# A two-layer transformer block on one core: out's products and the latent attention's projections laid between attention units

## The chip, the cores and the metric

The kernel runs on one core of a Trainium2 chip. The metric is the device time of one execution in microseconds (us); the time of a kernel is the median of its runs.

## The reference

One sequence of 256 tokens, width 1024, goes through two layers, all in fp32. Each layer is a mixer and a mixture of experts, with `x = layer_norm(ALPHA * x + h)` behind either.

- **Mixer of layer 0**: 16 heads of 64. Eight are *sliding* heads (window 128, with sinks). Eight are *NSA* heads, a gated sum of three branches: compressed keys, selected blocks (with 256 tokens all blocks are selected, so a causal attention), and a window of 512 (again causal). The 16 heads' outputs, 1024 columns, are multiplied by `w_out` (1024 x 1024).
- **Mixer of layer 1** (multi-head latent attention): x is projected to 384 + 256 + 32 columns; the first two are RMS-normed latents, from which `w_uq` gives q (16 heads of 64 + 32) and `w_ukv` gives keys without position (64 each) and values (64 each). The last 32 of q and of k are rotated by position; the 32 of k are shared by all heads. Causal attention, then `w_out`.
- **Experts**: 64 experts of inner width 256, six picked per token through groups, and one shared expert. All 64 experts' weights, three times 1024 KB each, are read in each layer, 2 x 201 MB of the 444 MB that the kernel moves.

## The kernel before

Tokens are worked in two blocks of 128 (`TC` = 2), the width in eight chunks of 128 (`KC`). `xrow` holds x by rows, `xcol` its transpose. Each engine has its instruction list in the order of the source and waits by semaphores; nothing is reordered by a planner, so the lists written out in `@block.tensor` (L887), `@block.scalar`, `@block.vector` (L1353) and `@block.sync` (L428) are the schedule. SyncE (SP) issues all DMAs, each behind the waits that stand before it.

**Memory.** `ring` has four slots of 3 MB, one expert each; in the mixers they hold weights and data of the mixer (slot 0 `win1`, then q by rows, `qn1`; slot 1 `w_ukv`; slot 2 `w_uq`; slot 3 latents and turned queries). `wbig` holds `w_out` (`wout`) in a mixer, 4 MB, and in `wbig`'s first half stand the first four units' probabilities of layer 0. PSUM has eight banks, `BANK[0..7]`, in pairs `PS[0..3]`. The expert weights are refilled by `refills` (L347, L350): gate and up of a slot once TensorE has used it (`gu_pe`), down likewise. Before the expert stage slots 0 to 3 and one kept expert are loaded: in layer 0 behind the projections, in layer 1 slot 2 after the q products, slot 1 after the kv products, slot 0 after the turned queries and keys; slot 3, the shared expert and the kept one in `mixture_loads` (L406), behind the last values.

**Attention units.** A unit is four heads by 128 queries. For unit u TensorE makes the scores (`pe_scores`, L572), VectorE masks them and takes the maximum (`soften`, L1465, L1468), ScalarE takes exponentials with sums (`act_exp`, L1134), VectorE normalises (`normalise`, L1545, L1551), TensorE turns the probabilities (`pe_turn_probs`, L613), ScalarE copies them out of PS[2] (`act_turned`, L1148), and TensorE multiplies by the values (`pe_values`, L598 and L586). Units of the first query block see 128 keys, those of the second 256. VectorE copies the heads' outputs to `attot`, and `pe_out_part` (L637) multiplies by `wout` into `OUT` = (PS[0], PS[3]), one for each token block, in two halves of 512 columns, each the sum of eight products over 128 rows.

**Layer 0** has 12 units: 0 to 3 sliding, 4 to 11 NSA. The sliding heads' outputs (rows 0 to 3 of `attot`'s eight chunks) are copied at L1494, ahead of unit 4. Units 4 to 11 are laid out by hand with the compressed branch between them (L531 to L557, softmax at L1529 to L1536, turned at L512, copied by ScalarE at L1282, which scores 9 wait for). out for token block 0 is laid between the last units, for block 1 in `pe_mixed`, eight products ahead of the turned columns of block 0 (L496) and eight behind. `mixed` (VectorE) adds each half to ALPHA times x (L1429), takes statistics (L1430), and `normed` (L1419, L1421) ends the layer norm, with the root from GpSimd (L1341).

**Layer 1** goes phase by phase: for each token block columns (L496) and the latent projection (L1038); RMS norms of both blocks; ten turns of the latents (L1050) and the rotated key part (L1055); six q products (L1064) and eight kv products (L1074), each copied out by ScalarE (L1305, L1308); 16 groups of turned keys and queries (L1089, L1091, copies L1313, L1315); then `pe_attention`, eight units in a pipeline (scores u, values u-3, turn u-2), with out's products of block 0 in the last three steps.

```python
for u in range(n + 3):
    if u < n: pe_scores(pe, 1, u)
    if u >= n: pe_out_part(pe, 1, 0, ...)
    if u >= 3: pe_values(pe, 1, u - 3)
    if 2 <= u <= n + 1: pe_turn_probs(pe, 1, u - 2)
```

Of the kernel before, what the change touches and what calls it, by code (L numbers as in the profile page):

```python
# [10 lines left out]
ALU = mybir.AluOpType  # L11
# [4 lines left out]
P = 128  # L16
S, D = 256, 1024
TC = S // P
# [57 lines left out]
def constants():  # L76
# [27 lines left out]
    for tc in range(TC):  # L104
# [22 lines left out]
       "sink_dve", "win1_in", "wuq_in", "wukv_in",  # L127
       "var_dve", "root_pool", "power_pool", "rms_dve", "cnt_pe", "cnt_act", "q_pe", "q_act", "kv_pe", "kv_act",
# [4 lines left out]
def bass_hybrid_block(nc, x, w_in0, sinks, pe_k, ck1, ck2, pe_v, cv1, cv2, w_out0, w_in1, q_norm,  # L133
# [3 lines left out]
    with ctx:  # L137
# [105 lines left out]
        s1 = [xt[:, 0:1024], xt[:, 1024:2048], arena[:, e0:e0 + 1024]]  # L243
# [67 lines left out]

        UNITS = [[unit0(n) for n in range(12)], [unit1(n) for n in range(8)]]
# [117 lines left out]
        def _(sp):  # L430
# [20 lines left out]
            norm_loads(sp, "mix", ln_mix_g, ln_mix_b, 0)  # L451
            sp.wait_ge(sem["pv_pe"], EARLY)
            sp.dma_start(wout, w_out0[0].rearrange("(c p) n -> p c n", p=P)).then_inc(sem["wout_in"], 16)
# [106 lines left out]
        def pe_scores(pe, L, u):  # L560

            U = UNITS[L][u]
            read = {0: None, 1: None, 2: 1, 3: 2, 4: 3, 5: 3, 6: 4, 7: 5, 8: 7, 9: None, 10: 8, 11: 9}[u] if L == 0 else u - 2
# [38 lines left out]
        def pe_turn_probs(pe, L, u):  # L602
# [6 lines left out]
            s = v(probs(L, u)[:, 0:R * w], j=R, k=w)  # L609
            po = v(PS[2][:, 0:R * w], j=R, k=w)  # L610
# [5 lines left out]
        def pe_attention(pe):  # L616
            n = len(UNITS[1])
            for u in range(n + 3):
                if u < n:
                    pe_scores(pe, 1, u)  # L620
                if u >= n:
                    if u == n:
                        pe.wait_ge(sem["wout_in"], BOTH["wout_in"] + 16)
                        pe.wait_ge(sem["o_dve"], BOTH["o_dve"] + 2)
                        pe.wait_ge(sem["max_dve"], BOTH["max_dve"] + 2 * n)
                    pe_out_part(pe, 1, 0, range((u - n) * 4, (u - n) * 4 + (4 if u < n + 2 else 8)))
                if u >= 3:
                    pe_values(pe, 1, u - 3)
                if 2 <= u <= n + 1:
                    pe_turn_probs(pe, 1, u - 2)  # L630

        OUT = (PS[0], PS[3])

        def pe_out_part(pe, L, tc, steps_):
            for i in steps_:
                half, c = i // KC, i % KC
                mm = pe.matmul(OUT[tc][:, half * 512:(half + 1) * 512], attot[L][:, c, tc * P:(tc + 1) * P],  # L637
                               wout[:, c, half * 512:(half + 1) * 512], start=c == 0, stop=c == KC - 1)
                if c == KC - 1:
                    mm.then_inc(sem["out_pe"], 1)  # L640

# [226 lines left out]
        def pe_mixed(pe, L):  # L868
# [3 lines left out]
            pe_out_part(pe, L, 1, range(KC))  # L872
            pe_columns(pe, st, 0, "lnmix_dve", TC * L)
            pe_out_part(pe, L, 1, range(KC, 2 * KC))
# [12 lines left out]
        def _(pe):  # L887
# [119 lines left out]
            pe_values(pe, 0, 6)  # L1007
# [3 lines left out]
            pe_values(pe, 0, 7)  # L1011
            pe_turn_probs(pe, 0, 8)
# [30 lines left out]
            for c in range(5):  # L1043
# [7 lines left out]
                if c % 2 or c == 4:  # L1051
                    mm.then_inc(sem["cnt_pe"], 1)
# [824 lines left out]
```

## Time and profile before

| | |
|---|---|
| median of 3 runs | 1320.17 us (1319.45 to 1320.90) |
| the profiled execution, its own time | 1318.97 us |
| its span in the trace | 1317.2 us |
| TensorE (PE) busy | 1202.3 us, 91% |
| VectorE (DVE) busy | 365.2 us, 28% |
| ScalarE (ACT) busy | 257.3 us, 20% |
| moved by DMA | 444.39 MB, mean 337 GB/s |
| mean granted TensorE clock | 0.965 of full |

The sum of a change is made against the profiled execution, which is 1.2 us below the median. In the trace the first mixer lies from 0 to about 192 us, the first expert stage from there to 662, the second mixer from 668 to 832, the second expert stage to the end. A record of a matmul in fp32 is half of a product of the source: each is two records. Busy shares of TensorE say little, since its durations overlap; the starts of successive records and the chain of waits tell its pace.

### The profile page before, as it was taken

How to read it: one execution, taken by the hardware profiler on the slowest of the kernel's cores; microseconds unless marked ns; L12 is line 12 of the kernel's file. 1: busy time of each engine (PE TensorE's matmuls, PEld its weight loads, DVE VectorE, ACT ScalarE, POOL GpSimd, SP SyncE). 2: the span in 40 equal slices, each digit the busy share in tenths (PEclk: the TensorE clock that was granted, in tenths of full speed). 3: DMA queues.
4: the chain of work that ended last, by engine and by line, in shares of the span. 5: the costliest groups of instructions: out<-in, count | busy, mean ns of one | idle time of the engine just before them, and what ended most of it. 6: DMA issues, size and time to landing. Idle time of an engine off the chain costs nothing.

```text
span 1317.2 us, 16007 instructions
## 1 busy us (share of the span) xinstructions
PE 1202.3 (91%) x6187; PEld 547.5 (42%) x6187; DVE 365.2 (28%) x741; ACT 257.3 (20%) x544; POOL 16.0 (1%) x22
## 2 busy tenths in 40 slices
PE   7989999999999998999878799999999999999984
PEld 3556453433434342434234555443434344343431
DVE  0575451212112121212142346321212122121213
ACT  1343221111111111111112632121111121111110
POOL 0000000000000000000010001000000000000000
PEclk9996999999999999999978889999999999999997
DMA  9345439999999999999963506699999999999992
GB/s 341 76 171 245 167 136 390 419 419 419 387 393 419 420 421 420 421 420 419 423 243 112 207 1 265 233 420 419 420 419 362 421 419 421 420 421 421 420 419 104
DMA packets 68881, 444.39 MB, mean 337 GB/s; under 512 B 7777, under 2 KB 12257, under 8 KB 18529
## 3 DMA queue, kind: packets, MB, share of 16 engines
q1 hardware_dynamic: 68832, 443.71, 83.3%
q8 instruction: 35, 0.57, 0.2%
q14 instruction: 14, 0.11, 0.0%
HBM read 442.63 MB, written 1.05 MB: 337 GB/s over the span
## 4 chain that ended last, share of the span: by engine, by line
PE 70%; DMA 19%; DVE 4%; ACT 3%; issue 2%; SPq 2%; POOL 1%; POOLq 0%; DVEq 0%
PE psum L780 28%; DMA ring<-in_expert_w_up 18%; PE psum L803 11%; PE psum L732 5%; PE psum L637 4%; PE psum L897 3%; PE psum L829 3%; PE psum L572 2%; PE psum L660 2%; DMA ring<-in_swa_nsa_w_in 2%; PE psum L1038 2%; PE psum L1064 1%; SPq L347 1%; PE psum L813 1%; PE psum L745 1%
## 5 line engine op out<-in xcount | busy, mean ns | idle before, releaser
L780 PE MATMUL psum<-ring,arena 128*64 128x512 f32 x2016 | 458.9, 601 | 31.4 <-DMA ring<-in_expert_w_up 31.4
L780 PEld LDWEIGHTS psum<-ring,arena 128*64 128x64 f32 x2016 | 156.3, 138 | 324.5 <-issue 271.3
L803 PE MATMUL psum<-ring,room 128*64 128x512 f32 x1008 | 233.8, 597 | 2.1 <-ACT room L1200 0.9
L1661 DVE TENSOR_TENSOR y_low<-psum,y_high 128x1024 fp32r<-128x1024 f32 x64 | 78.4, 1225 | 366.1 <-ACT y_high L1186 366.1
L1652 DVE SCALAR_TENSOR_TENSOR room<-room,arena,psum 128x256 f32<-128x256 f32 x64 | 30.7, 480 | 370.6 <-ACT room L1193 370.6
L803 PEld LDWEIGHTS psum<-ring,room 128*64 128x64 f32 x1008 | 75.8, 136 | 129.4 <-issue 119.9
L1186 ACT CAST y_high<-psum 128x1024 fp32r<-128x1024 f32 x64 | 64.8, 1012 | 252.2 <-PE psum L803 252.2
L1193 ACT ACTIVATE room<-psum 128x256 f32<-128x256 f32 x64 | 24.6, 385 | 418.9 <-PE psum L780 418.9
L829 PE MATMUL psum<-y_high,spread 32*128 32x512 f32 x512 | 65.7, 503 | 5.0 <-issue 4.8
L732 PE MATMUL psum<-onehot,x_high 128*128 128x256 f32 x256 | 65.7, 297 | 0.0
L732 PE MATMUL psum<-onehot,x_low 128*128 128x256 f32 x256 | 62.9, 283 | 0.0
L897 PE MATMUL psum<-ring,room 128*128 128x512 f32 x128 | 57.4, 598 | 2.5 <-DMA ring<-in_swa_nsa_w_in 1.7
L829 PE MATMUL psum<-y_low,spread 32*128 32x512 f32 x512 | 52.1, 395 | 0.0
L829 PEld LDWEIGHTS psum<-y_high,spread 32*128 32x128 f32 x512 | 24.8, 184 | 59.0 <-issue 55.8
L1643 DVE COPY arena<-psum 128x512 f32<-128x512 f32 x64 | 44.3, 692 | 17.7 <-PE psum L732 17.4
L732 PEld LDWEIGHTS psum<-onehot,x_high 128*128 128x128 f32 x256 | 48.3, 189 | 1.0 <-issue 0.5
L732 PEld LDWEIGHTS psum<-onehot,x_low 128*128 128x128 f32 x256 | 48.5, 189 | 0.5 <-issue 0.5
L813 PE MATMUL psum<-cst,room 128*128 128x128 f32 x128 | 27.6, 297 | 20.3 <-DVE room L1652 20.3
L1179 ACT COPY arena<-psum 128x512 f32<-128x512 f32 x64 | 37.6, 587 | 35.8 <-PE psum L732 35.6
L1200 ACT COPY room<-psum 128x256 f32<-128x256 f32 x64 | 23.9, 373 | 81.1 <-PE psum L813 81.1
L897 PEld LDWEIGHTS psum<-ring,room 128*128 128x128 f32 x128 | 23.4, 190 | 30.9 <-issue 27.3
L813 PEld LDWEIGHTS psum<-cst,room 128*128 128x128 f32 x128 | 12.9, 141 | 47.5 <-DVE room L1652 24.8
(232 smaller groups left out, 898.4 us busy)
## 6 DMA issues: line engine op xcount, KB each, us to landing
ring<-in_expert_w_down SPq DMA_DIRECT2D x126, 1024.0 KB, 16.5
ring<-in_expert_w_gate SPq DMA_DIRECT2D x122, 1024.0 KB, 14.6
ring<-in_expert_w_up SPq DMA_DIRECT2D x122, 1024.0 KB, 16.5
ring<-in_swa_nsa_w_in SPq DMA_DIRECT2D x8, 1036.0 KB, 13.7
room<-in_swa_nsa_w_out SPq DMA_DIRECT2D x1, 4096.0 KB, 14.1
ring<-in_expert_w_gate SPq DMA_DIRECT2D x8, 512.0 KB, 7.3
ring<-in_expert_w_up SPq DMA_DIRECT2D x8, 512.0 KB, 8.4
room<-in_mla_w_out SPq DMA_DIRECT2D x1, 4096.0 KB, 20.6
```

Source lines behind the costliest of these rows:

```text
L637: mm = pe.matmul(OUT[tc][:, half * 512:(half + 1) * 512], attot[L][:, c, tc * P:(tc + 1) * P], wout[:, c, half * 512:(half + 1) * 512], st ...
L732: mm = pe.matmul(got[:, :, tc, :], part[:, tc, c, :], onehot[:, tc, :, tc, :], start=part is xhi, stop=part is xlo)
L780: mm = pe.matmul(BANK[2][CAP * e:CAP * e + CAP, :], xg[:, c, 2 * j + e, :], expert(stored[e])[0][:, c], start=c == 0, stop=c == KC - 1)
L803: mm = pe.matmul(PS[0][CAP * e:CAP * e + CAP, half * 512:(half + 1) * 512], ht[:, c, CAP * e:CAP * e + CAP], expert(stored[e])[1][:, c, ha ...
L813: mm = pe.transpose(BANK[3][:, c * P:(c + 1) * P], hh[:, c, :], ident)
L829: mm = pe.matmul(ACC[tc][:, half * 512:(half + 1) * 512], spread[rows, j, tc * P:(tc + 1) * P], part[rows, half * 512:(half + 1) * 512], s ...
L897: return pe.matmul(part_bank(n, tc), xcol[:, c, tc * P:(tc + 1) * P], win0[:, c, n * 512:(n + 1) * 512], start=c == 0, stop=c == KC - 1)
L1179: nc.scalar.copy(xg[:, c, :, :], v(BANK[c % 3], e=GE, s=CAP)).then_inc(sem[f"xg_act{L}"], 1)
L1186: nc.scalar.copy(yhi, PS[0][:, :]).then_inc(sem[f"ya_act{L}"], 1)
L1643: V.tensor_copy(xg[:, c, :, :], v(BANK[c % 3], e=GE, s=CAP)).then_inc(sem[f"xg_dve{L}"], 1)
L1652: V.scalar_tensor_tensor(hh, byc(sg), gslot[:, j, 0:1], byc(BANK[2][:, DE:2 * DE]), ALU.mult, ALU.mult).then_inc(sem[f"h_dve{L}"], 1)
L1661: V.tensor_tensor(ylo, PS[0][:, :], yhi.bitcast(F32), ALU.subtract).then_inc(sem[f"yd_dve{L}"], 1)
```

## The change

In layer 0 the products of out over the sliding heads' four chunks are taken out of the end and made early, by `pe_out_early`, in four pieces (token block, half) of four products each into `BANK[5]`, between later units. VectorE adds each piece to ALPHA times x at once; at the end it adds the rest without ALPHA. `wout` is loaded in two halves, the early one at the first unit. In layer 1 the phases are taken apart: `FILLS` = 30 fills (6 q products, 8 kv products, 8 groups of four turned keys, 8 of four turned queries) rotate through three banks, and stand between the units of attention in orders written out for each engine; token block 0 runs ahead of block 1. The squares of the RMS norm, the scores' and probabilities' places and the loads' waits follow.

```diff
 SyncE
+            sp.wait_ge(sem["max_dve"], 2)
+            sp.dma_start(wout[:, 4:8, :], wo[:, 0:4, :]).then_inc(sem["wearly_in"], 16)
             sp.wait_ge(sem["pv_pe"], EARLY)
-            sp.dma_start(wout, w_out0[0].rearrange("(c p) n -> p c n", p=P)).then_inc(sem["wout_in"], 16)
+            sp.dma_start(wout[:, 0:4, :], wo[:, 4:8, :]).then_inc(sem["wout_in"], 16)
...
-            sp.wait_ge(sem["q_pe"], 6)
+            sp.wait_ge(sem["fill_pe"], 16)
             load_expert(sp, 1, 2, 2)
-            sp.wait_ge(sem["kv_pe"], 8)
+            sp.wait_ge(sem["fill_pe"], 26)
             load_expert(sp, 1, 1, 1)
-            sp.wait_ge(sem["qk_pe"], BOTH["qk_pe"] + 16)
+            sp.wait_ge(sem["fill_pe"], FILLS)
+            sp.wait_ge(sem["ptr_pe"], BOTH["ptr_pe"] + 6)
             load_expert(sp, 1, 0, 0)
 TensorE
+        FILL_BANK = (BANK[2], BANK[3], BANK[5])
             if L:
-                return PS[u % 2]
+                return BANK[u % 2] if u < 4 else PS[u > 4]
...
+                pe.wait_ge(sem["kfull_dve"], U["qc"] + 1)
+                pe.wait_ge(sem["fill_act"], (8, 11, 15, 18, 22, FILLS, FILLS, FILLS)[u])
...
+        def pe_q(pe, k, tc, n):
+            pe.wait_ge(sem["cnt_act"], 2 * tc + 1)
+            pe.wait_ge(sem["wuq_in"], 16)
+            if k >= 3:
+                pe.wait_ge(sem["fill_act"], k - 2)
+            for c in range(3):
+                mm = pe.matmul(FILL_BANK[k % 3], ct1[:, c, tc * P:(tc + 1) * P], uq[:, c, n * 512:(n + 1) * 512],
+                               start=c == 0, stop=c == 2)
+            mm.then_inc(sem["fill_pe"], 1)
+        def pe_turn_queries(pe, k, tc, hg):
+            pe.wait_ge(sem["qrope_dve"], tc + 1)
+            pe.wait_ge(sem["fill_act"], k - 2)
+            for i in range(4):
+                h = 4 * hg + i
+                mm = pe.transpose(FILL_BANK[k % 3][0:DQK, i * P:(i + 1) * P], qn1[:, tc, h * DQK:(h + 1) * DQK], ident)
+            mm.then_inc(sem["fill_pe"], 1)
...
+        def pe_out_early(pe, tc, half):
+            if (tc, half) == (0, 0):
+                pe.wait_ge(sem["wearly_in"], 16)
+                pe.wait_ge(sem["qk_act"], 6)
+            else:
+                pe.wait_ge(sem["early_dve"], 2 * tc + half)
+            pe.wait_ge(sem["o_dve"], tc + 1)
+            for c in range(4):
+                mm = pe.matmul(BANK[5], attot[0][:, c, tc * P:(tc + 1) * P], wout[:, 4 + c, half * 512:(half + 1) * 512],
+                               start=c == 0, stop=c == 3)
+            mm.then_inc(sem["early_pe"], 1)
...
             pe_compressed_values(pe)
+            pe_out_early(pe, 0, 0)
             pe_scores(pe, 0, 6)
             pe_turn_probs(pe, 0, 4)
             pe_compressed_scores(pe)
             pe_scores(pe, 0, 7)
+            pe_out_early(pe, 0, 1)
             pe_values(pe, 0, 4)
             pe_turn_probs(pe, 0, 5)
             pe_scores(pe, 0, 8)
+            pe_out_early(pe, 1, 0)
             pe_values(pe, 0, 5)
             pe_turn_probs(pe, 0, 6)
             pe_compressed_turn(pe)
             pe_scores(pe, 0, 9)
+            pe_out_early(pe, 1, 1)
...
-            pe_out_part(pe, 0, 0, range(3))
+            pe_out_part(pe, 0, 0, range(2))
             pe_values(pe, 0, 9)
-            pe_out_part(pe, 0, 0, range(3, 6))
+            pe_out_part(pe, 0, 0, range(2, 4))
             pe_turn_probs(pe, 0, 10)
+            pe_values(pe, 0, 10)
+            pe_out_part(pe, 0, 0, range(4, 6))
+            pe_turn_probs(pe, 0, 11)
             pe_out_part(pe, 0, 0, range(6, 8))
-            pe_values(pe, 0, 10)
-            pe_out_part(pe, 0, 0, range(8, 10))
-            pe_turn_probs(pe, 0, 11)
-            pe_out_part(pe, 0, 0, range(10, 16))
             pe_values(pe, 0, 11)
 VectorE
-                    link(V.scalar_tensor_tensor(r, r, ALPHA, OUT[tc][:, cols], ALU.mult, ALU.add))
+                    if L:
+                        link(V.scalar_tensor_tensor(r, r, ALPHA, OUT[tc][:, cols], ALU.mult, ALU.add))
+                    else:
+                        link(V.tensor_tensor(r, r, OUT[tc][:, cols], ALU.add))
...
+            def out_early(tc, half):
+                dve.wait_ge(sem["early_pe"], 2 * tc + half + 1)
+                r = xrow[:, tc, half * 512:(half + 1) * 512]
+                mark(V.scalar_tensor_tensor(r, r, ALPHA, BANK[5], ALU.mult, ALU.add), "early_dve")
```

`pe_kv` and `pe_turn_keys` are made like `pe_q` and `pe_turn_queries` (two products, four turns). `pe_out_part` takes four chunks a half in layer 0 and eight in layer 1, and so does `pe_mixed`. VectorE's `out_early(0,0)` stands behind `normalise` of unit 5, the next three behind those of 6, 7 and 8. TensorE's new order in layer 1 (columns and projections first; a number is a fill, `s`, `t`, `v` scores, turned probabilities and values of a unit, `o` a count of out's products):

```
columns 0, project 0 (512), columns 1, project 0 (160), project 1 (512), turn latents 0, project 1 (160),
q0 q1 q2 kv3, turn latents 1, kv4 keys5 kv6 queries7 keys8 kv9 queries10,
s0 q11 s1 q12 keys13 queries14 t0 s2 q15 v0 t1 keys16 queries17 kv18 s3 v1 kv19 t2 keys20 queries21
v2 kv22 t3 keys23 queries24 v3 kv25 keys26 queries27 s4 keys28 queries29
o3 s5 o3 t4 s6 v4 o2 t5 s7 v5 o3 t6 v6 o3 t7 o2 v7
```

ScalarE and VectorE follow the same order with their copies, exponentials, norms and rotations. VectorE masks and takes the maximum of unit u+1 before it normalises unit u, from unit 4 on.

## Rows read from the trace of the kernel before

**Rows 1.** Stretches: length, busy us and count by engine, granted clock, DMA share, GB/s
```profile
88.90:149.80 60.90, 53.81 (x237) 34.29 (x237) 31.30 (x66) 23.24 (x84) 0.00 (x0) 0.78 0.49 200
...
200.00:660.00 460.00, 431.52 (x2360) 176.18 (x2360) 89.73 (x165) 72.69 (x123) 0.00 (x0) 0.99 1.01 415
668.50:699.90 31.40, 26.10 (x93) 16.03 (x93) 9.66 (x26) 6.57 (x17) 2.92 (x3) 0.83 0.51 184
...
739.60:790.30 50.70, 43.71 (x240) 29.42 (x240) 25.37 (x36) 21.87 (x73) 0.00 (x0) 0.87 0.16 63
```

**Rows 2.** Waits of the DMA queue: total us, times, longest
```profile
SPq L347 <- PE psum L780: 366.8, 58, 10.0
...
SPq L347 <- PE psum L586: 50.6, 1, 50.6
SPq L453 <- PE psum L598: 45.9, 1, 45.9
```

**Rows 3.** Chain of waits, end of the first mixer: start, us, what
```profile
143.60 5.15 PE psum L637 x12
...
150.55 7.13 PE psum L637 x16
157.69 0.89 PE psum L496 x8
158.58 6.88 PE psum L637 x16
```

**Rows 4.** Timeline, first mixer: start, us, engine, line, operation, idle before and releaser
```profile
113.51 1.11 PE L512 MATMUL psum<-cst,ring 128*128 128x128 f32 x4 [2.44 <-DVE ring L1536]
...
115.30 3.77 PE L572 MATMUL psum<-arena 64*128 64x256 f32 x8 [0.68 <-ACT ring L1282]
...
149.81 0.69 DVE L1498 COPY room<-psum 128x512 f32<-128x512 f32 x1 [13.71 <-PE psum L598]
...
155.43 1.28 DVE L1421 SCALAR_TENSOR_TENSOR x_rows<-x_rows,small,lnp 128x1024 f32<-128x1024 f32 x1 [0.53 <-POOL small L1341]
```

**Rows 5.** Timeline of TensorE, second mixer
```profile
671.21 11.09 PE L1038 MATMUL psum<-ring,room 128*128 128x512 f32 x32 [0.68 <-ACT room L1103]
...
684.01 9.28 PE L1038 MATMUL psum<-ring,room 128*128 128x512 f32 x32 [0.83 <-ACT room L1103]
...
731.08 3.68 PE L1089 MATMUL psum<-cst,arena 128*64 128x128 f32 x32 [0.68 <-ACT arena L1308]
...
745.48 1.06 PE L572 MATMUL psum<-arena,ring 96*128 96x128 f32 x8
...
754.76 1.89 PE L572 MATMUL psum<-arena,ring 96*128 96x256 f32 x8
...
769.00 1.09 PE L586 MATMUL psum<-arena 128*64 128x128 f32 x16 [0.54 <-ACT arena L1148]
770.03 1.09 PE L613 MATMUL psum<-cst,arena 128*128 128x128 f32 x8
```

**Rows 6.** Stretches that bear on the granted clock, columns as in rows 1
```profile
91.30:94.80 3.50, 1.16 (x8) 0.96 (x8) 2.97 (x7) 2.58 (x13) 0.00 (x0) 0.97 1.02 410
94.80:121.40 26.60, 22.07 (x76) 15.51 (x77) 14.68 (x37) 9.99 (x42) 0.00 (x0) 0.50 0.89 367
...
731.00:738.70 7.70, 7.25 (x64) 6.81 (x64) 0.00 (x0) 6.99 (x16) 0.00 (x0) 1.00 0.96 368
...
660.00:674.50 14.50, 7.23 (x28) 3.93 (x29) 10.89 (x15) 1.17 (x2) 3.04 (x2) 0.54 0.80 271
```

**Rows 7.** Timeline of VectorE and ScalarE, a late unit of the second mixer
```profile
763.46 1.23 DVE L1465 SCALAR_TENSOR_TENSOR room<-psum,cst 128x1024 f32<-128x1024 f32 x1 [2.05 <-PE psum L572]
...
764.72 1.22 DVE L1468 TENSOR_REDUCE small<-room 128x4 f32<-128x1024 f32 x1
...
765.98 0.51 ACT L1134 ACTIVATE room<-room,small 128x256 f32<-128x256 f32 x1 [3.34 <-DVE small L1468]
...
767.96 0.99 ACT L1148 COPY arena<-psum 128x1024 f32<-128x1024 f32 x1
```

More of the change, by code:

```diff
@@ new lines, in pe_kv, with pe_turn_keys @@
+        def pe_kv(pe, k, tc, n):
+            pe.wait_ge(sem["cnt_act"], 2 * tc + 2)
+            pe.wait_ge(sem["wukv_in"], 16)
+            pe.wait_ge(sem["fill_act"], k - 2)
+            for c in range(2):
+                mm = pe.matmul(FILL_BANK[k % 3], ct1[:, 3 + c, tc * P:(tc + 1) * P], ukv[:, c, n * 512:(n + 1) * 512],
+                               start=c == 0, stop=c == 1)
+            mm.then_inc(sem["fill_pe"], 1)
+        def pe_turn_keys(pe, k, tc, hg, kv):
+            pe.wait_ge(sem["fill_act"], max(k - 2, kv + 1))
+            for i in range(4):
+                h = 4 * hg + i
+                mm = pe.transpose(FILL_BANK[k % 3][0:NOPE, i * P:(i + 1) * P], kv1[:, tc, h * 128:h * 128 + NOPE], ident)
+            mm.then_inc(sem["fill_pe"], 1)
@@ L1093, in _, with compress @@
-            pe.wait_ge(sem["qk_act"], BOTH["qk_act"] + 16)
-            pe.wait_ge(sem["kfull_dve"], 1)
-            pe_attention(pe)
+            def compress(tc, n, w):
+                for c in range(KC):
+                    mm = pe.matmul(PS[2 + tc][:, n:n + w], xcol[:, c, tc * P:(tc + 1) * P], win1[:, c, n:n + w],
+                                   start=c == 0, stop=c == KC - 1)
+                mm.then_inc(sem["proj_pe1"], 1)
+            pe_columns(pe, 2, 0, "lnffn_dve")
+            columns_ready(pe, 2, 0)
@@ L1096, in _ @@
+            pe_turn_probs(pe, 1, 5)
+            pe_scores(pe, 1, 7)
+            pe_values(pe, 1, 5)
+            pe_out_part(pe, 1, 0, range(8, 11))
+            pe_turn_probs(pe, 1, 6)
+            pe_values(pe, 1, 6)
+            pe_out_part(pe, 1, 0, range(11, 14))
+            pe_turn_probs(pe, 1, 7)
+            pe_out_part(pe, 1, 0, range(14, 16))
+            pe_values(pe, 1, 7)
             pe_mixed(pe, 1)
@@ new lines, in queries_turned @@
+            def queries_turned(k, tc, hg):
+                act.wait_ge(sem["fill_pe"], k + 1)
+                nc.scalar.copy(qt1[0:DQK, 4 * hg:4 * hg + 4, tc * P:(tc + 1) * P],
+                               v(FILL_BANK[k % 3][0:DQK, :], h=4, t=P)).then_inc(sem["fill_act"], 1)
+            latent(0)
+            latent_turned(0)
+            latent(1)
+            q_out(0, 0, 0)
+            q_out(1, 0, 1)
+            q_out(2, 0, 2)
+            kv_out(3, 0, 0)
+            latent_turned(1)
@@ L1815, in _, with rms @@
             dve.wait_ge(sem["small1_in"], 32)
-            for tc in range(TC):
+            def rms(tc):
                 dve.wait_ge(sem["proj_act1"], 2 * tc + 1)
@@ new lines, in _ @@
+            U = UNITS[1]
+            rms(0)
+            key_rope(0)
+            rms(1)
+            key_rope(1)
+            keys_filled(0)
+            query_rope(0)
+            soften(1, 0)
+            soften(1, 1)
+            normalise(1, U[0], 0)
+            keys_filled(1)
+            soften(1, 2)
+            normalise(1, U[1], 1)
+            query_rope(1)
+            normalise(1, U[2], 2)
+            soften(1, 3)
+            heads_out(0)
+            normalise(1, U[3], 3)
+            heads_out(1)
@@ L1846, in _ @@
+            soften(1, 4)
+            soften(1, 5)
+            normalise(1, U[4], 4)
+            soften(1, 6)
+            normalise(1, U[5], 5)
+            soften(1, 7)
+            normalise(1, U[6], 6)
+            heads_out(2)
+            normalise(1, U[7], 7)
+            heads_out(3)
             mixed(1)
```

323 lines of the change are left out of this document (187 added, 136 removed).

## The prediction

> **What bounds the kernel now.** I read the stretches first [rows 1]. In the expert stage of a layer (200 to 660 us) the DMA engines are full, at 415 GB/s; in the mixers they move 63 to 200 GB/s. So each layer is two things in a row: a mixer, in which the weights can't flow since their slots hold the mixer's own data, and then a stream of weights. The queue's waits show how the two hang together [rows 2]: SP waits on TensorE's gate and up products before it refills a slot, and through the second mixer it waited once for 50.6 us, for the values' products of L586, with nothing to move. The stream starts when the mixer has ended, so a microsecond off a mixer should be one off the kernel, provided that the first slots are full by then. The mixers are therefore what to read, and in them the granted clock: 0.78 of full over the end of the first, 0.83 and 0.87 in the first and last part of the second [rows 1].
>
> **The unit of work.** One product of 128x512 in fp32 is two records of 0.43 us at the full clock (2.4 GHz): 16 records took 6.88 us [rows 3].
>
> **First mixer, the end.** Of out's 32 products, 16 (those of the sliding heads) leave the end. Between the last scores and the end of the last values (149.8) eight go, 16 records, 6.9 us; the 12 records before the last values alone are 5.15 us [rows 3]. The new order puts the values of unit 10 right behind their turn, and ScalarE's copy of 1.0 us (the one at 767.96 is its like [rows 7]) stands between the two, so 1.1 comes back: 5.8 saved. Behind 149.8 token block 1 has 16 + 16 records, with the turned columns between (7.13, 0.89, 6.88 us) [rows 3]. Half of each goes. But the columns wait for the layer norm of block 0, which begins with the copy at 149.81 and ends with the pass that starts at 155.43 and takes 1.28 [rows 4], at 156.7. Today the products cover that; with half of them TensorE stands still for 2.6 us, and what was busy till 165.5 ends at 156.7 + 0.9 + 3.4 = 161.0. Saved 4.5.
>
> **First mixer, where the four pieces go.** Each is 8 records, 3.44 us. Piece 1 stands before scores 6, where TensorE now idles for the normalised probabilities (it works 1.16 of the 3.5 us from 91.3 [rows 6]): hidden, all but 0.2. Piece 2 comes between scores 7 and scores 8, on the path: 3.4. Piece 3 falls into the compressed branch's softmax, where TensorE waits 2.44 us for VectorE [rows 4], and delays unit 6's turn by about 1 us. ScalarE takes that turn's copy, then the exponentials of unit 8 (2.0 us, as from 765.98 to 767.96 [rows 7]), and only then the copy at L1282 on which scores 9 wait; that wait, 0.68 us today [rows 4], becomes 2.6: cost 1.9. Piece 4 is on the path again: 3.4. Together 8.7. The four additions on VectorE (0.69 us each, as the pass over 512 columns at 149.81 [rows 4]) fall into its idle time (31 us busy of 61 [rows 1]); in place of the scaled addition at the end stands a plain one of the same length.
>
> Against this stands the clock. From 94.8 to 121.4 the first mixer runs at 0.50 (the 1.2 GHz level), after 3.5 us in which TensorE worked 1.16 us [rows 6]. Walking the same order with durations at the full clock brings the last scores 7.7 us sooner; that is what the low level costs. Piece 1 fills the very gap ahead of the fall, so I take this visit as gone, and allow two shorter ones at the two gaps of 2.6 us that the new order has. A short visit is priced by the first projection of the second mixer, which took 11.09 us against 9.28 for its twin: 1.8 [rows 5]. Sum of the first mixer: 5.8 + 4.5 - 8.7 + 7.7 - 3.6 = 5.7 us saved.
>
> **Second mixer.** It takes 121.8 us, 668.5 to 790.3. TensorE's own work in it, at the full clock: columns 1.8; projections of the latents 2 x 9.28 [rows 5]; their turns 12 x 0.13, by the eight of a unit in 1.03 to 1.09; 68 records of q and kv at 0.43, 29.2; 64 turns of keys and queries, 7.4 (32 took 3.68 [rows 5]); scores 4 x 1.06 and 4 x 1.9; turns of probabilities 4 x 1.03 and four of half that; values the same [rows 5]; out's first block, 32 records, 13.8. In all 97. The other 25 us are low clock and waits. The change makes no product cheaper; it lays the work of one dependency under the waits of another. I walked the three queues in the new order with these durations and a late unit's chain [rows 7]: masking 1.23 and maximum 1.22, the exponentials 2.0, and a reciprocal and a product of 1.6 together (the product a pass over 1,024 columns as the masking is). What still stands still: 0.8 before the first projection (0.68 in its row [rows 5]); 1.2 in short waits for copies among the fills; then in units 4 to 7, where no fill is left, the normalisation of unit u stands behind the masking of unit u+1, which waits for scores u+1, against 2.6 us of out's products: 1.6, 1.4, 0.6, and 1.1 for a turned copy. Sum 6.7. The low clock at the start (0.54 from 660 to 674.5 [rows 6]) stays: 1.8. So 97 + 6.7 + 1.8 = 105.5, ending at 774.0, 16.3 sooner. For one more low visit I take off 1.8: 14.5 saved. The same walk in the old order, with the low visits put in, ends within 2 us of 790.3, so I trust it to that.
>
> **The DMA queue.** Out's early weights (2 MB) are asked for before the wait of 45.9 us that stood ahead of all of them [rows 2]; behind that wait nothing else is late. The expert of slot 0 is now asked for when unit 5's probabilities have been turned, about 757 us, and 3.1 MB at 415 GB/s are 7.6 us: full by 767, before 774. Were it late by its whole length, 7.6 would come back. SP's earlier requests stand behind fills 16 and 26 and gate nothing else.
>
> **The rule on transposes.** The 64 turns of keys and queries ran with the clock granted at 1.00 throughout (731 to 738.7) [rows 6]. The Trainium skill, "TensorE: Matmul & The Clock Gate", Part 4 (PE-mode transpose), says that the full clock does not engage for transpose mode. By it, these turns among the fills would run at half the rate, some 7 us more; this trace disagrees for its turns behind dense products, and I go by the trace.
>
> **Sum.** 5.7 + 14.5 = 20.2 us. The profiled execution took 1318.97 us for a span of 1317.2; less 20.2 it is 1298.8, and on the median of 1320.17 it is 1300.0.
>
> **Rivals.** (A) *The clock holds everywhere*: neither the 3.6 nor the 1.8 is paid: 5.4 more saved, 1294.6. For it: piece 1 and the fills close the gaps that came before today's falls. Against: gaps of 2.6 us remain, and one of 2.3 came before the fall at 94.8 [rows 6]. Chance 0.13.
> (B) *The first mixer gives back what it gains.* From 94.8 to 121.4 TensorE was busy 22 of 26.6 us and the clock stayed at 0.50 [rows 6], so small products do not bring it back at once. If it falls where the 16 narrow products of the compressed scores stand, piece 2 costs 6.9 in place of 3.4 and the scores round it double: 4 to 6 us off; 1305. Chance 0.15.
> (C) *ScalarE holds the fills.* Three banks rotate, and a fill may start only when the copy two before it is out. ScalarE is in order, so a copy behind four exponentials waits 1.5 us. With some five of the groups late at this price, the second mixer gives 7 to 8 less: 1308. Against: ScalarE is busy only 22 of 50.7 us even in the attention part [rows 1]. Chance 0.08.
> (D) *No gain arrives*: the weights' stream, not the mixer, sets the end, for instance since slot 0 or the shared weights land late by as much as the mixer gained. Against: 63 GB/s in the attention part and the 50.6 us wait. About 1320, chance 0.03.
> (E) *Slower, by the clock in the second mixer.* Fills of 0.5 us between turns that wait for copies could keep TensorE at 1.2 GHz through the fill stretch, as in 94.8 to 121.4. Work at the low level costs half its time extra. It decides from 40 us of low level beyond today's on: that eats the 20.2. At 55 us, some two thirds of the fills and units, it is +27 against -20: 1327. Against: the fills are dense products for 29 of their 50 us. Chance 0.03.
>
> **How the numbers follow.** The forecast, 1300, has 0.58, with 1296 to 1304 as its own range (each visit of the clock 1.8, the walk good to 2). To hold 8 in 10 the range takes in A at its lower side, with 2 us for the walk, and B, and part of C: 1292 to 1308. A measurement of this kernel tells 0.2% (2.6 us) from no change. Faster by more than that: the forecast, A, B, C and most small mishaps, 0.94; within 0.2%: D, 0.03; slower: E, 0.03.
>
> **What would show it.** In the changed kernel's profile: the end of the second mixer's values some 14 to 16 us nearer to its start at the columns; the stretch after the first expert stage begins 5 to 6 us sooner; clock near 1.00 between 95 and 110 us; a wait of some 2.6 us for the copy of the turned compressed probabilities, and one of like size before the columns of the first mixer; DMA again at 415 GB/s in the expert stages, unchanged in length. I am wrong if the expert stages grow as the mixers shrink (D), if scores 8 of the first mixer still show 3.7 us (B), or if TensorE's waits in the fill stretch name ScalarE's exponentials (C).

## The result and the profile after

The changed kernel took 1302.84 us (four runs, 1298.41 to 1304.80) against 1320.54 for the kernel before on the same chip: a ratio of 0.9861, with an interval of 0.9839 to 0.9883, so 15 to 21 us faster. Measured again beside a later group of experiments it took 1300.86 against 1321.21, ratio 0.9851 (0.9832 to 0.9869). The profiled execution was one of 1303.12 us, with a span of 1301.3; before, 1318.97 and 1317.2. The forecast was 1300.0.

Where the time went, by the starts of five stretches in the two traces (us):

| | first expert stage starts | columns of the second mixer | its last values end | second expert stage starts | span |
|---|---|---|---|---|---|
| before | 191.93 | 668.56 | 790.25 | 832.41 | 1317.2 |
| after | 191.17 | 668.91 | 774.02 | 816.20 | 1301.3 |
| gained in the stretch that ends there | 0.8 | -1.1 | 16.6 | 0.0 | -0.3 |

The second mixer gave 16.6 us, the first 0.8, and the two expert stages took them over almost unchanged. The sum, 15.9, is the difference of the spans.

The page of the changed kernel, parts 1 and 2 (busy time; granted clock and transfer rate in 40 slices of 32.5 us):

```profile
PE 1194.9 (92%) x6187; PEld 540.2 (42%) x6187; DVE 368.0 (28%) x746; ACT 256.9 (20%) x546; POOL 16.0 (1%) x22
...
PEclk9997999999999999999979999999999999999997
...
GB/s 344 143 146 211 125 176 375 418 420 419 402 376 420 421 419 421 420 420 421 421 339 35 194 164 213 309 419 420 420 418 361 421 419 420 421 420 421 421 419 91
```

The mixers are still the two stretches in which few bytes move (slices 2 to 6 and 21 to 26), and the only slices below 9 in the clock are in them, one in each, beside the last slice of all. The stretches of the changed kernel that matter, with the columns of [rows 1]:

```profile
98.80:104.60 5.80, 5.80 (x21) 4.64 (x21) 2.37 (x7) 0.51 (x4) 0.00 (x0) 0.50 1.00 418
...
118.90:125.20 6.30, 6.30 (x12) 3.54 (x13) 2.68 (x4) 0.00 (x0) 0.00 (x0) 0.50 0.01 3
...
159.90:163.30 3.40, 3.40 (x6) 1.34 (x5) 2.02 (x1) 1.52 (x3) 0.00 (x0) 0.50 1.02 429
668.90:693.30 24.40, 23.72 (x87) 14.55 (x88) 7.68 (x16) 4.20 (x11) 2.22 (x2) 0.87 0.57 206
693.30:739.10 45.80, 44.71 (x212) 26.11 (x211) 18.43 (x36) 25.82 (x72) 0.70 (x1) 1.00 0.24 92
739.10:774.00 34.90, 30.83 (x170) 19.10 (x168) 15.71 (x17) 14.26 (x40) 0.00 (x0) 1.00 0.46 181
```

In the second mixer the low level is gone but for its start: 80.7 us (45.8 + 34.9) at 1.00, where [rows 1] had 0.87 over the attention part. TensorE stands still for 0.7 + 1.1 + 4.1 = 5.8 us of 105.1. With the two outer stretches of [rows 1], the middle one of the kernel before gives the comparison:

```profile
699.90:739.60 39.70, 37.76 (x132) 20.07 (x132) 6.36 (x9) 16.04 (x31) 0.00 (x0) 0.97 0.44 166
```

Before, TensorE was busy 26.1 + 37.8 + 43.7 = 107.6 us of 121.8 and stood still for 14.2; now it is busy 99.3 and stands still for 5.8, with the same products. So about half of the 16.6 us (8.4) are waits, and the other half (8.3) is busy time that the low clock had stretched. In the first mixer the one long stay at 1.2 GHz [rows 6] has become three short ones; such a stay is called a *visit*.

The chain of waits of the changed kernel through the first mixer (start, us, what; L707 is a piece of out's early products, L585 scores, L565 the narrow products of the compressed scores, L693 out's late products):

```profile
91.30 3.63 PE psum L707 x8
...
97.84 3.12 PE psum L565 x16
100.96 2.00 PE psum L585 x8
102.97 4.78 PE psum L707 x8
...
110.84 3.63 PE psum L707 x8
...
116.26 1.97 ACT ring L1228 x8
118.23 0.48 ACT ring L1368
118.70 0.04 issue
118.75 3.67 PE psum L585 x8
122.41 5.29 PE psum L707 x8
...
158.38 1.16 PE psum L504 x8
159.54 5.15 PE psum L693 x8
```

Pieces 1 and 3 take 3.63 us; piece 2 and piece 4, on which the clock is low for a part, take 4.78 and 5.29. The eight records after the columns take 5.15, where half of L637's 6.88 [rows 3] would be 3.44. Ahead of scores 9 the chain shows just what it waits for: the four exponentials of unit 8 on ScalarE, each with the reading of its sum (x8, 1.97), and then the copy L1368.

TensorE in the second mixer, timeline of the changed kernel (start, us, line, shape, idle time before and its releaser):

```profile
671.55 8.96 PE L1108 MATMUL psum<-ring,room 128*128 128x512 f32 x16 [0.68 <-ACT room L1197]
...
750.84 1.09 PE L628 MATMUL psum<-cst,room 128*128 128x128 f32 x8 [1.34 <-DVE room L1693]
...
757.58 1.09 PE L628 MATMUL psum<-cst,ring 128*128 128x128 f32 x8 [0.98 <-DVE ring L1693]
...
766.51 1.09 PE L599 MATMUL psum<-arena 128*64 128x128 f32 x16 [1.10 <-ACT arena L1242]
...
772.90 1.09 PE L599 MATMUL psum<-arena 128*64 128x128 f32 x16
```

Most of the waiting that is left is that of the late units: the normalisation behind the next unit's mask (L1693, 1.34 and 0.98), and one turned copy (1.10).

### The profile page after: what moved, and what is told of

It is laid out like the page before. It is cut to its first block, busy times and chain, and to the rows that moved or that the text cites. A ratio compares the mean times of both kernels' runs of the same rounds, so it can differ in the third digit from the quotient of the medians.

```text
span 1301.3 us, 16051 instructions
## 1 busy us (share of the span) xinstructions
PE 1194.9 (92%) x6187; PEld 540.2 (42%) x6187; DVE 368.0 (28%) x746; ACT 256.9 (20%) x546; POOL 16.0 (1%) x22
## 3 DMA queue, kind: packets, MB, share of 16 engines
HBM read 442.63 MB, written 1.05 MB: 341 GB/s over the span
## 4 chain that ended last, share of the span: by engine, by line
PE 70%; DMA 20%; DVE 4%; ACT 2%; issue 2%; SPq 2%; POOL 1%; POOLq 0%; DVEq 0%
PE psum L849 28%; DMA ring<-in_expert_w_up 18%; PE psum L872 11%; PE psum L801 5%; PE psum L967 3%; PE psum L898 3%; PE psum L693 3%; PE psum L585 2%; PE psum L729 2%; DMA ring<-in_swa_nsa_w_in 2%; PE psum L1108 2%; PE psum L707 1%; SPq L351 1%; PE psum L882 1%; PE psum L638 1%
## 5 line engine op out<-in xcount | busy, mean ns | idle before, releaser
L849 PEld LDWEIGHTS psum<-ring,arena 128*64 128x64 f32 x2016 | 157.0, 139 | 326.2 <-issue 272.8
```

What stands on the lines that cost most here:

```text
L849: mm = pe.matmul(BANK[2][CAP * e:CAP * e + CAP, :], xg[:, c, 2 * j + e, :], expert(stored[e])[0][:, c], start=c == 0, stop=c == KC - 1)
```

## The experiments

Ten runs: nine other kernels, and the changed kernel itself once more. They were measured in three groups, each on a chip of its own, and each ratio stands to the kernel before on that same chip (1321.13, 1321.61 and 1321.21 us in the three groups). Differences between the experiments are read from their traces, stretch by stretch, since the intervals are about 5 us wide. Traces vary too: the first expert stage, from its start to the columns of the second mixer, took from 474.5 to 478.6 us in the twelve of them.

| kernel | median us | ratio (interval) | first expert stage starts |
|---|---|---|---|
| first mixer's part alone (`m1only`) | 1317.52 | 0.9981 (0.9965 to 0.9997) | 189.90 |
| second mixer's part alone (`m2only`) | 1303.16 | 0.9872 (0.9851 to 0.9892) | 192.69 |
| the changed kernel, products that nothing reads in three gaps (`keepwarm`) | 1296.25 | 0.9811 (0.9788 to 0.9833) | 183.87 |
| the changed kernel, ScalarE's copy first (`copyfirst`) | 1296.51 | 0.9820 (0.9798 to 0.9842) | 186.06 |
| the changed kernel, columns behind out's products (`outfirst`) | 1298.71 | 0.9826 (0.9808 to 0.9845) | 187.57 |
| the changed kernel, pieces later by one place (`latepieces`) | 1307.58 | 0.9894 (0.9876 to 0.9911) | 195.06 |
| three repairs of the order (`real`) | 1289.79 | 0.9767 (0.9748 to 0.9786) | 178.88 |
| and unread products at the layers' seam (`best`) | 1287.33 | 0.9744 (0.9727 to 0.9761) | 179.20 |
| and normalisation ahead of the mask (`normfirst`) | 1288.05 | 0.9743 (0.9723 to 0.9763) | 179.45 |
| the changed kernel again (`after_again`) | 1300.86 | 0.9851 (0.9832 to 0.9869) | 188.16 |

### Each half of the change alone

The edits are the two halves of the diff: `m1only` has layer 0's early products and two loads of `wout` and leaves layer 1 in phases; `m2only` has the fills and leaves layer 0.

> The first mixer's part alone, the second mixer as before. Theory: the changed kernel's whole gain is the second mixer's; here the first expert stage starts within 2 us of before (191.9), since three visits at the low clock (ahead of scores 7, at scores 9, behind the columns) cost some 3 us each and eat what the moved products save; the time is 1317 to 1321. Rival (the chain of the first mixer gained as forecast and the expert stage lost it): the stage starts at 186 to 187, and the time is 1314 to 1316 or the stage is 5 us longer.

> The second mixer's part alone, the first mixer as before. Theory: the second mixer takes 105 to 107 us from its first columns to its last values, and the time is 1303 to 1306: the two parts add up, and this one is nearly all. Rival (part of the gain needs the first mixer's change, for instance by when the slots are full): 1308 or more.

The second mixer's part alone gave 0.9872, what the whole change gave. Its mixer took 106.1 us (668.34 to 774.42), and its first mixer what it took before (192.69 against 191.93). The first mixer's part gave 0.4 to 4.6 us, 2.0 in its trace. So nearly all of the gain is the second mixer's, and within the intervals the two parts add up: 0.19% and 1.28% against 1.39% for the whole. The trace of `m1only` has two visits, not the expected three: one that begins at the compressed scores' narrow products and one at scores 9, and none behind the columns.

### The clock: products that nothing reads

```diff
             pe.transpose(BANK[2][:, 0:NCMP], kcn[0:NCMP, :], ident[0:NCMP, 0:NCMP]).then_inc(sem["kct_pe"], 1)
+            for i in range(2):
+                pe.matmul(BANK[7], attot[0][:, i % 4, 0:P], wout[:, 4 + i % 4, 0:512], start=True, stop=True)
             pe.wait_ge(sem["kct_dve"], 1)
```

Three more stand ahead of scores 9, and three ahead of the columns of token block 0.

> The changed kernel with products that nothing reads, laid in the first mixer's three gaps: two of 128x512 ahead of the compressed scores, three ahead of scores 9, three ahead of the columns of token block 0. Theory (the low clock is what the first mixer lost): the granted clock stays at 1.00 from 90 to 165 us, scores 9 take 1.9 and piece 4 takes 3.5 us; the first expert stage starts at 184 to 187 and the time is 5 to 7 us below the changed kernel's, though 7 us of work were added. Rival (the pieces themselves fill the path, the clock is a bystander): the added products make the first mixer up to 1 us longer, and the time is the same or above.

Eight products of 0.86 us, 6.9 us of work, were added into free banks, and nothing else was changed. The ratio to the kernel before fell to 0.9811 (0.9788 to 0.9833), from 0.9861 (0.9839 to 0.9883) for the changed kernel. The chain of waits of this kernel, first mixer (L567 narrow products, L587 scores, L709 pieces, L695 out's late products):

```profile
99.09 1.70 PE psum L567 x16
100.79 1.08 PE psum L587 x8
101.88 3.63 PE psum L709 x8
...
116.51 1.99 PE psum L587 x8
118.50 3.63 PE psum L709 x8
...
153.96 3.45 PE psum L695 x8
```

All three visits are gone; the granted clock is 1.00 from 86 to 165. The first cost (3.12 - 1.70) + (2.00 - 1.08) + (4.78 - 3.63) = 3.5 us, the second (3.67 - 1.99) + (5.29 - 3.63) = 3.3, the third 5.15 - 3.45 = 1.7: 8.5 together. The added products mostly stand where TensorE waited anyway, so 7.3 us arrive at the first expert stage (191.17 to 183.87). The low clock, not the moved work or its waits, is what ate most of the first mixer's gain. The transfers are not behind it: in the changed kernel they ran at 418 GB/s in the first visit and at 3 in the second, and here at 426 from 99 to 105 with the clock at 1.00.

### The wait ahead of scores 9

```diff
             act_turned(act, 0, 6)
-            act_exp(act, 0, 8)
             act.wait_ge(sem["cpt_pe"], 1)
             nc.scalar.copy(cpt, v(BANK[3], u=4, q=P)).then_inc(sem["cpt_act"], 1)
+            act_exp(act, 0, 8)
```

> The changed kernel with ScalarE's copy of the turned compressed probabilities put ahead of the exponentials of unit 8. Theory (that order is what makes scores 9 wait 2.67 us): the wait falls to 0.7, TensorE's gap with it, the clock no longer falls there in most executions, so scores 9 and piece 4 take 1.9 and 3.5 in place of 3.67 and 5.29: 2 us of wait and up to 3.5 of clock, 3 to 5 us in all. Rival (the copy waits for something else, or the later units wait for unit 8's exponentials instead): 0 to 1 us.

The chain of waits of this kernel (L565, L585, L707 as in the changed one, L1367 the copy):

```profile
98.03 3.27 PE psum L565 x16
101.30 2.00 PE psum L585 x8
103.30 6.32 PE psum L707 x8
...
118.13 0.50 ACT ring L1367
118.63 0.04 issue
118.67 1.99 PE psum L585 x8
120.66 3.63 PE psum L707 x8
```

The four exponentials are off the chain (1.97), and scores 9 and piece 4 run at the full clock (3.3): 5.3 us for a copy moved ahead of them. The first visit stays, and costs more than the 3.5 us of the changed kernel (3.27, 2.00 and 6.32 against 1.70, 1.08 and 3.63: 5.2); in its place the third, of 1.7, did not come in this execution. So the second visit belongs to the 2.67 us wait, and the first does not. The other traces say the same of the second: `m1only`, `outfirst`, `latepieces` and the changed kernel's second profile keep that wait (2.67 to 2.68 us) and have a visit of 3.3 us there, and `real`, `best` and `normfirst`, which have not, have none.

### The wait ahead of the columns

```diff
-            pe_columns(pe, st, 0, "lnmix_dve", TC * L)
+            if L:
+                pe_columns(pe, st, 0, "lnmix_dve", TC * L)
             pe_out_part(pe, L, 1, range(n, 2 * n))
+            if L == 0:
+                pe_columns(pe, st, 0, "lnmix_dve", TC * L)
```

> The changed kernel with, in layer 0, the turned columns of token block 0 behind all eight products of out for block 1, and the statistics of block 1 ahead of the low part of x of block 0 on VectorE. Theory (halving the cover of the layer norm's wait cost 2.6 us of stillness and then a visit at the low clock): no gap before the columns, the product after it no longer at 0.50, the layer norm of block 1 starts 2 to 4 us sooner, 3 to 5 us off the changed kernel. Rival (the wait was hidden by the next one, the routing's chain on VectorE): under 1 us.

VectorE's norm of block 1 goes ahead of `x_low` of block 0 in the same way. From the end of the last values to the first expert stage it took 35.5 us (152.11 to 187.57); the same stretch takes 38.0 in `m1only`, which had no visit behind the columns, and 39.8 in the changed kernel, which had one. So the order is worth 2.5 us by itself. The wait before the columns alone doesn't bring a visit each time: in `m1only`, `copyfirst`, `latepieces` and the changed kernel's second profile the same 2.5 us of stillness stands there, and the clock stays at 1.00. The first two visits are there (piece 2 5.91 us, piece 4 6.42). The kernel's time lies 2.1 and 4.1 us below the two medians of the changed one, at the lower end of the 3 to 5 expected or under it, and its interval overlaps that of the changed kernel; the 2.5 is a reading of traces.

### The pieces one place later

```diff
             pe_compressed_values(pe)
-            pe_out_early(pe, 0, 0)
             pe_scores(pe, 0, 6)
...
             pe_scores(pe, 0, 7)
-            pe_out_early(pe, 0, 1)
+            pe_out_early(pe, 0, 0)
```

and so on: behind scores 7, 8, 9 and 10, and VectorE's additions with them.

> The changed kernel with the four early pieces one place later each: behind scores 7, 8, 9 and 10 in place of compressed values and scores 7, 8, 9. Theory (piece 1 is hidden where it stands, and what it saves is the visit at the low clock that begins at 94.8 in the kernel before): the clock falls again near 95 us and stays at 0.50 till a dense piece has passed; the last scores of the first mixer end 3 to 6 us later than in the changed kernel, and the time is 3 to 5 us above it. Rival (a piece costs the same wherever it stands, and the clock falls anyway): within 1 us of the changed kernel.

The clock falls at about 94.2, close to where it fell before the change, and stays at 0.50 until about 107.9, within piece 1. The last values end at 157.0, in place of 151.4 and 150.1 in the two profiles of the changed kernel and 151.9 in `m1only`. So the order with piece 1 in the gap ahead of scores 6 is worth 5 to 7 us against this one, with the same products in both; all four pieces were moved, so the share of piece 1 alone is not shown.

### Repairs, and a version faster than both

`real` takes the order of `copyfirst` and of `outfirst`, and splits piece 1 (`pe_out_early` now takes a range of chunks), so that real work fills the gap that `keepwarm` filled with unread products:

```diff
             pe_compressed_values(pe)
-            pe_out_early(pe, 0, 0)
+            pe_out_early(pe, 0, 0, range(2))
...
             pe.transpose(BANK[2][:, 0:NCMP], kcn[0:NCMP, :], ident[0:NCMP, 0:NCMP]).then_inc(sem["kct_pe"], 1)
+            pe_out_early(pe, 0, 0, range(2, 4))
             pe.wait_ge(sem["kct_dve"], 1)
```

> The changed kernel with three edits, no product more or less: the copy of the turned compressed probabilities ahead of unit 8's exponentials, the columns of block 0 behind all of out, and the last two products of piece 1 moved behind the turned compressed keys, into the 1.07 us gap ahead of the narrow products. Theory: the visits at the low clock ahead of scores 7, at scores 9 and behind the columns go, the first expert stage starts at 182 to 185 (191.2 in the changed kernel), and the time is 1291 to 1295. Rival (each fix only moves the next wait up): no better than the copy alone, 1296 to 1298.

Its stretches, with the columns of [rows 1], and two pieces of its chain of waits (L708 pieces, L566 narrow products):

```profile
86.00:155.00 69.00, 63.78 (x324) 37.97 (x324) 46.14 (x90) 28.80 (x93) 3.70 (x4) 1.00 0.56 227
155.00:192.00 37.00, 34.98 (x168) 19.19 (x169) 20.06 (x74) 9.13 (x16) 0.83 (x3) 1.00 0.60 215
```

```profile
96.71 1.91 PE psum L708 x4
98.62 1.70 PE psum L566 x16
```

The clock is at 1.00 from 86 to 192, without a product that nothing reads. The first expert stage starts 12.3 us sooner than in the changed kernel (178.88 against 191.17) and 13.1 sooner than before, more than the 182 to 185 that was expected. Visits, exponentials and the order of the columns, as priced above, would be 8.5 + 2.0 + 2.5 = 13.0.

`best` adds eight products of `ident` by `cst`, which nothing reads, at the end of the first expert stage, two ahead of the last combination and six ahead of the layer norm's wait:

```diff
+            for i in range(0 if L else 2):
+                pe.matmul(BANK[2], ident, cst[:, P:P + 512], start=True, stop=True)
             for turn in range(2):
                 pe_combine(pe, L, n_groups * GP - 1, 1, turn, True)
```

> The kernel of the run with the three edits, and at the seam of the layers products that nothing reads: two while TensorE waits for the last pair's high part, six while it waits for the layer norm. Theory (the second mixer's first projection pays some 2 us for the low clock in which it starts): that projection takes 6.9 us in place of 9, and 2 us more come off: 1289 to 1293. Rival (the added products overrun the layer norm's wait of 6 us, at the low clock, or the clock falls all the same): the same as without, or 1 to 4 us more.

The first projection then starts at the full clock; the timeline and the stretches of this kernel:

```profile
657.01 1.17 PE L504 MATMUL psum<-cst,x_rows 128*128 128x128 f32 x8 [0.80 <-DVE x_rows L1572]
658.88 7.13 PE L1117 MATMUL psum<-ring,room 128*128 128x512 f32 x16 [0.71 <-ACT room L1206]
```

```profile
155.00:158.00 3.00, 3.00 (x5) 1.34 (x4) 3.00 (x3) 1.12 (x1) 0.00 (x0) 0.50 1.02 423
```

7.13 us against 8.96 in the changed kernel, and 1.17 for the turned columns ahead of it (L504) against 1.97: 2.6 for the low start. Against `real`, whose second mixer starts at the low level (1.97 and 9.49), the stretch from these columns to the last values took 102.5 us in place of 105.6, so 3.1 less. One short visit came back in the first mixer, at 155 (and at the same products in `normfirst`), where `real` had none. The medians are 2.5 us apart and the intervals overlap, so by their times `real` and `best` are not told apart; both are faster than the changed kernel and the kernel before.

`normfirst` is `best` with the late units' order on VectorE turned round (normalise unit u, then mask unit u+1):

```diff
+            normalise(1, U[4], 4)
             soften(1, 5)
-            normalise(1, U[4], 4)
+            normalise(1, U[5], 5)
             soften(1, 6)
-            normalise(1, U[5], 5)
+            normalise(1, U[6], 6)
             soften(1, 7)
-            normalise(1, U[6], 6)
```

> The kernel with the three edits and the products at the seam, and in the second mixer's units 4 to 7 VectorE normalises unit u before it masks unit u+1. Theory (turns of units 4, 5 and 6 wait 1.3, 1.0 and 0 us because the normalisation stands behind a masking that waits for the next scores): the turn of unit 4 no longer waits, and 1 to 3 us come off the second mixer, 1284.5 to 1286.5. Rival (the masking then comes late, and the next unit's exponentials with it): within 1 us of 1287.3.

The timeline of this kernel (L600 values of units 4, 5 and 6):

```profile
735.03 1.09 PE L600 MATMUL psum<-arena 128*64 128x128 f32 x16 [0.43 <-ACT arena L1251]
...
741.01 1.09 PE L600 MATMUL psum<-arena 128*64 128x128 f32 x16 [0.37 <-ACT arena L1251]
...
746.99 1.09 PE L600 MATMUL psum<-arena 128*64 128x128 f32 x16 [1.24 <-ACT arena L1251]
```

The waits for VectorE of 1.34 and 0.98 are gone, others of 0.43 and 0.37 for turned copies took their place, the third grew from 1.10 to 1.24, and from the first projection to the last values 98.6 us pass against 100.6 in `best`. In the median that 2 us can't be seen: 1288.05 against 1287.33 is where the rival expected it, not the 1284.5 to 1286.5 of the theory. Whether the order helps stays open.

### The changed kernel once more

> The changed kernel itself once more, beside the others of this call on one chip. Theory (the phase of the clock's falls decides some microseconds from execution to execution): 1298 to 1305, with a spread between executions of 5 us or more, and in its trace the clock falls after the same waits as in the first profile (ahead of scores 7, at scores 9, behind the columns), if not after all three. Rival (the first profile was one bad draw): one fall or none, and a time below 1299.

In its profiled execution (1298.23 us) the chain of waits reads:

```profile
98.07 1.97 PE psum L565 x16
100.04 1.08 PE psum L585 x8
101.13 5.33 PE psum L707 x8
...
117.45 2.82 PE psum L585 x8
120.28 6.14 PE psum L707 x8
```

Two visits, and none behind the columns. The first costs 1.7 us, on piece 2 alone (the narrow products and scores 7 ran at a granted clock of 1.00), the second 3.3: 5.0 in place of 8.5, and the first expert stage starts at 188.16 instead of 191.17. The same program, with the same waits, thus varies by the number of visits and their length, and this 3 us is most of what lies between its two profiled times (4.9).

## Why the prediction was right, and the term that was not

**The total** came to within 3 us, inside the forecast's own range (1296 to 1304), with the right cause for most of it. The sum was 5.7 + 14.5; the trace shows 0.8 + 16.6, less 1.4 that the expert stages gave back. That is partly luck: the first mixer gave 4.9 less than forecast and the second 2.1 more, and without what the second gave beyond its sum the kernel would have stood outside that range, near rival B's 1305. Of the signs that the prediction named, two did not come: the clock was at 0.50 from 98.8 to 104.6, not near 1.00, and the stretch after the first expert stage began at 668.91, not 5 to 6 us sooner than 668.56. Both lie in the first mixer.

**Second mixer: right.** The walk gave 105.5 us without the extra visit, ending at 774.0; it took 105.1 and ended at 774.02. Its parts agree too: waits of 6.7 forecast, 5.8 measured; of these 1.6, 1.4, 0.6 and 1.1 in units 4 to 7 came as 1.34, 0.98, none and 1.10; 1.2 among the fills as 1.1; 0.8 ahead of the first projection as 0.68. The low start cost 2.6, not 1.8 (8.96 and 1.97 against 7.13 and 1.17 in `best`). The allowance of 1.8 for one more visit was not needed. So TensorE had about 97 us of work (105.1 - 5.8 - 2.6), as summed, and the 16.6 us that the interleaving took away were waits and low clock.

**First mixer, the end: right.** From the last scores to the end of the last values 15.3 us pass (136.11 to 151.40) against 21.0 (128.80 to 149.79), so 5.7 saved, where 5.8 was forecast. Behind that 4.5 less one visit of 1.8 was forecast, 2.7; it was 2.4, with a wait of 2.51 us for the layer norm where 2.6 was expected, and a visit of 1.7. (`m1only`, without that visit, saved 4.1.)

**First mixer, the pieces: the step that failed** is "I take this visit as gone, and allow two shorter ones at the two gaps of 2.6 us". By the sum the last scores should have ended 8.7 - 7.7 + 1.8 = 2.8 us later; they ended 7.3 later (136.11 against 128.80). (The four costs of the pieces named in the prediction, 0.2, 3.4, 1.9 and 3.4, add up to 8.9 and not to 8.7, which changes little.) The waits were as foreseen (2.67 us ahead of scores 9). But a visit there cost 3.3 us, not 1.8, since all of it lay on scores 9 and piece 4; the price of 1.8 was read from the first projection alone, and left out the turned columns ahead of it, which ran at the low level too (1.97 us in the changed kernel, against 1.05 for their twins at 680.35); and a visit of 3.5 us came that the sum didn't have, at the narrow products of the compressed scores. Together 6.8 in place of 1.8; with the 1.7 at the columns, 8.5 in place of 3.6: 4.9 more, as much as the first mixer fell short by. That the rest was right is shown by `keepwarm` and `real`. With no visit the sum puts the last scores 8.7 - 7.7 = 1.0 later than before, and `keepwarm` has them 1.7 later, with its added products; without the wait for the copy (1.9) it puts them 0.9 sooner, and `real` has them 0.7 sooner (128.12 against 128.80). So the 7.7 of the gone visit arrives, and the stage begins 8 and 13 us sooner than before.

**The rivals.** B, at a chance of 0.15, is what happened in the first mixer: it named the place (the narrow products, piece 2 at more than 3.4), and its price of 4 to 6 us off the first mixer was right, 4.9. Its details were not: piece 2 took 4.78 and not 6.9, scores 8 took 1.92 and not the 3.7 that was to be its sign, and part of the 4.9 lay at scores 9. The measured 1302.84 is a little nearer to its 1305 than to 1300; what holds the time inside the forecast's range is that the second mixer gave more than its sum. A, the clock held everywhere, did not come with this change, but the order can be had: `real`. C did not come: 1.1 us of waits in the fill stretch, of which the profile lays 0.32 to a copy of ScalarE that stood behind exponentials, and the second mixer lost nothing. D is refuted: what the mixers gave reached the end, within 1.4 us. E did not come: the clock was 1.00 through the fills.

**The queue** held as argued. Its waits in the changed kernel, for the q products of the fills, the turned probabilities and the kv products:

```profile
SPq L351 <- PE psum L638: 25.8, 1, 25.8
...
SPq L488 <- PE psum L628: 19.0, 1, 19.0
...
SPq L351 <- PE psum L648: 13.9, 1, 13.9
```

The 50.6 us wait [rows 2] is broken up, slot 0 is asked for at 758.8, and its 3.1 MB are in by 768, before 774.0. Most slices of the expert stages still show 418 to 421 GB/s.

**The rule on transposes.** The 64 turns of keys and queries, now in groups of four between dense products, lie between 705.0 and 741.9 (56 of them before 739.1), at a granted clock of 1.00. The Trainium skill, "TensorE: Matmul & The Clock Gate", Part 4 (PE-mode transpose), has the full clock not engage for transpose mode; this trace disagrees again, now for turns mixed with products, and the 7 us that the rule would have cost did not appear. The same page of the Trainium skill, Part 1 (HAM oscillation), holds that a kernel whose matmuls pause for data drops to the low level again and again, and advises a loop order that keeps TensorE fed; `real` agrees: an order alone took away the three visits, 8.5 of its 12.3 us.

## What to carry to other kernels

Fill a wait with work that the kernel owes anyway, and choose the wait not by its length alone but by what stands behind it: dense products right behind a gap pay for a low clock in full, here 3.3 us behind a wait of 2.7, in each of five traces. When a product is moved ahead of a copy on which TensorE waits, look at what the copy's engine has queued before it; a copy put ahead of four exponentials on ScalarE was worth 5 us. And walk the queues of all engines in the new order with measured durations: here that gave waits and ends to within 1 us, while the clock, which no such walk holds, was nearly the whole error.

## What the runs showed of the hardware

- Products that nothing reads can pay: with 6.9 us of them the kernel took 6.6 us less than the first measurement of the changed one (1296.25 against 1302.84) and 4.6 less than the second. The chips differ, and against the second the intervals just touch (0.9788 to 0.9833, 0.9832 to 0.9869); the traces put 7.3 and 4.3 us at the start of the first expert stage (183.87 against 191.17 and 188.16).
- The clock can fall within narrow work. In the changed kernel it fell to 0.50 at 98.8, on 16 products of 30 columns behind a gap of 1.07 us, though TensorE was busy 11.6 of the 12.8 us from 86.0 to 98.8. In the other profiled execution it fell only behind those products and scores 7, between 101 and 102.
- In these kernels one short visit cost 1.7 to 5.2 us, the one long one before the change 7.7 by the prediction's walk, an estimate. Length alone doesn't tell which gap brings one: left open, the gap of 1.07 us ahead of the narrow products had a visit in each of five traces, the wait of 2.67 ahead of scores 9 in each of five, and the wait of 2.51 ahead of the columns in one of five. Two executions of one program differ by it, by some 3 us in this mixer.
- A product of 128x512 in fp32 in these pieces took 0.91 us (3.63 for four), not the 0.86 of the long rows of L637 [rows 3].
